# Second block of a channel mixer in seven products, with its first down product moved ahead of it

## The chip, the cores and the metric

The kernel runs on one core of one Trainium2 chip. The metric is the device time of one execution in microseconds (us); a median of three runs is given. A core has TensorE (matmuls, written PE in the profile; PEld is its weight load), VectorE (DVE), ScalarE (ACT), GpSimd (POOL) and SyncE (SP), which here only issues the loads of weights. The engines run side by side and each takes its instructions in the written order; they meet at semaphores.

## The reference, cut to what matters

The reference is two layers of a hybrid diffusion backbone: a token mixer (retention and neighbourhood attention), then a channel mixer, each behind norms and a modulation. Width is 1024, and 512 latent and 128 context tokens go through the same weights, so 640 tokens in all. The change touches the channel mixer alone:

```
def swiglu(h, wg, wu, wd):
    return (jax.nn.silu(h @ wg) * (h @ wu)) @ wd
...
hf = modulate(rmsnorm(x, n_pre_ffn), sh2, sc2)
return x + g2[:, None, :] * rmsnorm(swiglu(hf, w_ffn_gate, w_ffn_up, w_ffn_down), n_post_ffn)
```

wg and wu are 1024 x 2816, wd is 2816 x 1024.

## The kernel before

**Numbers in two parts.** Every operand of a matmul is a float32 that was split into a rounded high part and a low rest. A product is three matmuls (high by high, high by low, low by high). ScalarE makes the high part of a 128x1024 slab of weights (`split`, L1207) and VectorE the low part (`split`, L1696); both engines do the same for the activations.

**Blocks.** The 2816 hidden channels are cut into 11 blocks of 256. A block needs two gate and two up columns of 128 channels (each 1024 deep, for 640 tokens), then silu(gate) * up, split again into `hidh` and `hidl`, then a down product: five tiles of 128 tokens, each 60/5 = 12 matmuls of 512 columns, added up by VectorE in `mix`. Per block, six slabs of weights come by SyncE's queue: four for gate and up, two for down.

**Columns and sevens.** In the first two blocks (`SEVEN = 2`) each column is done plainly (`column`): 8 chunks of depth, 2 halves of 320 tokens, 3 matmuls, 48 matmuls of 320 columns. In the other nine blocks a pair of columns is done by a Strassen-like scheme (`seven`): seven products of quarters, each 4 x 3 matmuls of 320 columns, 84 in place of 96. `quarters(n, ...)` writes product n of pair r into one of four PSUM banks in turn, so product n+4 needs the bank of product n back: `seven_copied` for product 4 (ScalarE has copied product 0), `seven_added` 1 and 2 for products 5 and 6 (VectorE has added products 1 and 2).

What the seven products need beside the matmuls: three sums of weights per pair (`pair_sums`, VectorE, L2247 to L2252), the high and low parts of both slabs and of the sums (`pair_high` parts 0, 1, 2 on ScalarE, `pair_low` parts 0, 1, 2 on VectorE), and, once per layer, four sums of token quarters (`sum_of_tokens` 0 to 2 and `last_sum_of_tokens` on VectorE, L2191 to L2203; their high parts `token_sums` on ScalarE, L1563; their low parts `low_of_tokens` on VectorE, L1706).

**Order.** The order is written out by hand on each engine. TensorE: the four columns of block 0 (partly before all tokens are there, `first_columns`), the four columns of block 1, down of block 0, then for each later block its two pairs and the down of the block before it. VectorE makes the token sums beside the columns of block 1; the pair sums, low parts and last token sum of pair 0 and the sums of pair 1 stand beside the down of block 0. After the adds and the multiplication that end a pair of pairs (`seven_block`), VectorE's loop over the five down tiles (L2337) holds the low parts of the next pair (after tiles 0, 1 and 2) and the sums of the pair behind it (after tile 3).

The code that says which product waits for what, in `seven`:

```
pe.wait_ge(w_lo[slot[i + 1]], turn_of[i + 1])
pe.wait_ge(ts_ready, 4 * l + 4)
pe.wait_ge(seven_copied, r + 1)
quarters(4, s3, t3_)
pe.wait_ge(seven_added, 7 * r + 1)
quarters(5, a12, b21)
```

Of the kernel before, what the change touches and what calls it, by code (L numbers as in the profile page):

```python
# [7 lines left out]
P = 128  # L8
# [35 lines left out]
SEVEN, SIX = 2, 6  # L44
# [81 lines left out]
def build(nc, x_in, w_main, w_first, w_ada, params, decay, state_in, ctx_k, ctx_v, biases, ccol, cvec,  # L126
# [3 lines left out]
    with ctx:  # L130
# [365 lines left out]
        def _(pe):  # L496
# [189 lines left out]
            for l in range(DEPTH):  # L686
# [291 lines left out]

                def down(b):
                    pe.wait_ge(hid_ready, downs.value(1) * 2)  # L980
                    weights = [slab(512)[1:] for _ in range(2)]
                    for t in range(TILES):
                        u = U.take()
                        U.give(down_tile(u, b, t, weights, True, True))
                    slab_over(2)
                    downs.add()

                def seven(r):
# [31 lines left out]
                    pe.wait_ge(ts_ready, 4 * l + 4)  # L1020
# [4 lines left out]
                    pe.wait_ge(seven_added, 7 * r + 2)  # L1025
                    quarters(6, a22, t4_)
                    slab_done.extend([(seven_done, 7 * (r + 1))] * 2)

                def gate_up(b):
                    if b < SEVEN:  # L1030
                        for _ in range(4):
                            column()
                    else:
                        for n in range(2):
                            seven((b - SEVEN) * 2 + n)
# [161 lines left out]
        def _(act):  # L1197
# [93 lines left out]
            for l in range(DEPTH):  # L1291
# [273 lines left out]
                def gate_up(b, more=4):  # L1565
                    for n in range(2):
                        third = b == 0 and n == 1
                        if third:
                            act.wait_ge(bank_ready, 2 * l + 2)
                        else:  # L1570
                            u = U.get()

                        act.wait_ge(hid_ready, hids.count)
                        if third:
                            act.activation(sig[:, 0:CUT], sc[0][:, 0:CUT], ACT.Silu)
                            act.activation(sig[:, CUT:T], sc[1][:, 0:T - CUT], ACT.Silu).then_inc(bank_free, 1)
                        else:
                            for of, part in whole(u, sig[:, :], b == 0 and n == 0):
                                a = act.activation(part, of, ACT.Silu)
                            U.release(a)  # L1580
                        if more == 4:
                            split()
                        U.add()
                        U.wait_released(1)
                        act.activation(hidh[:, b % 2, n, :], sig[:, :], ACT.Copy).then_inc(hid_hi, 1)
                        hids.add()
                        if more == 4:
                            split()
                        else:
                            if n == 0:  # L1590
                                split(2)
                            token_sums(((0, 1), (3,))[n])

# [20 lines left out]

                def seven_block(b):
# [5 lines left out]
                    split(2)  # L1621
# [18 lines left out]
                gate_up(0)  # L1640
                for b in range(1, FB):
                    if b < SEVEN:
                        gate_up(b, 2 if b == SEVEN - 1 else 4)
                    else:
                        seven_block(b)
                    if b == SEVEN - 1:
                        pair_high(0, 0)
                        for t in range(TILES):
                            u = U.get()
                            U.release(act.activation(mix[:, t, :], flat(u[:, :, :]), ACT.Copy))  # L1650
                            if t == 0:
                                pair_high(0, 1)
                                pair_high(0, 2)
                            if t == 2:
                                token_sums((2,))
                    elif b < FB - 1:
                        U.add(TILES)
# [28 lines left out]
        def _(dve):  # L1686
# [220 lines left out]
            for l in range(DEPTH):  # L1907
# [302 lines left out]
                def gate_up(b, more=4):  # L2210
                    for n in range(2):
                        third = b == 0 and n == 1
                        if not third:
                            U.add()
                        if more == 4:
                            split()
                        elif n == 0:
                            sum_of_tokens(0)
                            sum_of_tokens(1)
                        u = U.get()  # L2220
                        if third:
                            dve.wait_ge(bank_free, 2 * l + 2)
                        else:
                            U.wait_released(1)
                        for part, to in whole(u, sig[:, :], b == 0 and n == 0):
                            a = dve.tensor_tensor(to, part, to, ALU.mult)
# [268 lines left out]
```

## Time and profile before

| what | value |
|---|---|
| median of 3 runs | 2127.77 us (2127.35 to 2129.45) |
| the profiled execution's own time | 2126.99 us |
| its span, first to last instruction | 2125.2 us |
| TensorE busy | 2097.1 us, 99% of the span |
| VectorE busy | 1545.4 us, 73% |
| ScalarE busy | 931.0 us, 44% |
| channel mixer of the first layer, about | 642 to 1060 us |
| channel mixer of the second layer, about | 1687 to 2118 us |

The profile is of one execution, so sums of its durations are made against 2126.99 us; the median lies 0.8 us above that. In a timeline each row has start, duration, engine, line, operation, the tiles written and read, shape and count, and in brackets the idle time before it with what ended it. Starts of matmuls are the pace of TensorE; their printed durations overlap, because they are pipelined.

### The profile page before, as it was taken

How to read it: one execution, taken by the hardware profiler on the slowest of the kernel's cores; microseconds unless marked ns; L12 is line 12 of the kernel's file. 1: busy time of each engine (PE TensorE's matmuls, PEld its weight loads, DVE VectorE, ACT ScalarE, POOL GpSimd, SP SyncE). 2: the span in 40 equal slices, each digit the busy share in tenths (PEclk: the TensorE clock that was granted, in tenths of full speed). 3: DMA queues.
4: the chain of work that ended last, by engine and by line, in shares of the span. 5: the costliest groups of instructions: out<-in, count | busy, mean ns of one | idle time of the engine just before them, and what ended most of it. 6: DMA issues, size and time to landing. Idle time of an engine off the chain costs nothing.

```text
span 2125.2 us, 33748 instructions
## 1 busy us (share of the span) xinstructions
PE 2097.1 (99%) x13874; PEld 1997.5 (94%) x13874; DVE 1545.4 (73%) x2467; ACT 931.0 (44%) x1482; POOL 101.6 (5%) x195
## 2 busy tenths in 40 slices
PE   7999999999999999999999999999999999999998
PEld 6999999899989999999899999999999899999997
DVE  5688767777756787887877776755854668787786
ACT  5655432476344432332475554235744544233332
POOL 0000001110000000000000000001100000000000
PEclk9999999999999999999999999999999999999999
DMA  7334355424333222222433333532233312222223
GB/s 306 113 116 129 105 169 174 143 93 147 101 134 115 80 80 80 80 80 86 162 132 119 110 112 132 168 127 78 86 119 130 129 60 80 80 80 85 95 80 139
DMA packets 63098, 246.05 MB, mean 116 GB/s; under 512 B 7777, under 2 KB 8065, under 8 KB 60257
## 3 DMA queue, kind: packets, MB, share of 16 engines
q1 hardware_dynamic: 42336, 158.55, 21.5%
q0 software_dynamic: 20608, 85.35, 11.4%
q8 instruction: 110, 1.80, 0.4%
q14 instruction: 44, 0.35, 0.1%
HBM read 230.20 MB, written 13.66 MB: 115 GB/s over the span
## 4 chain that ended last, share of the span: by engine, by line
PE 94%; DVE 3%; ACT 2%; DMA 1%; issue 0%; DVEq 0%; SPq 0%
PE unit L501 11%; PE unit L502 11%; PE unit L503 11%; PE unit L513 10%; PE unit L516 10%; PE unit L514 10%; PE sc L501 4%; PE sc L502 4%; PE sc L503 4%; PE tp L501 4%; PE tp L502 4%; PE tp L503 4%; PE tp L860 1%; PE sc L836 1%; PE unit L887 1%; PE unit L886 1%
## 5 line engine op out<-in xcount | busy, mean ns | idle before, releaser
L1696 DVE TENSOR_TENSOR wl<-raw,wh 128x1024 fp32r<-128x1024 f32 x204 | 246.9, 1221 | 127.6 <-ACT wh L1207 125.7
L513 PE MATMUL unit<-hmh,wh 128*128 128x320 f32 x1120 | 337.8, 309 | 0.8 <-DVE vl L1706 0.4
L514 PE MATMUL unit<-hml,wh 128*128 128x320 f32 x1120 | 337.3, 309 | 0.0
L516 PE MATMUL unit<-hmh,wl 128*128 128x320 f32 x1120 | 255.3, 309 | 0.0
L1207 ACT ACTIVATE wh<-raw 128x1024 fp32r<-128x1024 f32 x204 | 210.1, 1050 | 98.7 <-DMA raw<-w_main 98.6
L1798 DVE CUSTOM_DVE_ANT_0 junk<-ada,csb,par 128x1024 f32<-128x1024 f32 x160 | 205.5, 1285 | 28.8 <-DMA ada<-w_ada 9.0
L513 PEld LDWEIGHTS unit<-hmh,wh 128*128 128x128 f32 x1120 | 210.2, 188 | 1.2 <-issue 1.2
L514 PEld LDWEIGHTS unit<-hml,wh 128*128 128x128 f32 x1120 | 210.3, 188 | 0.0
L516 PEld LDWEIGHTS unit<-hmh,wl 128*128 128x128 f32 x1120 | 187.1, 188 | 0.0
L501 PE MATMUL unit<-wh,hmh 128*128 128x256 f32 (+1 forms) x544 | 178.9, 329 | 1.5 <-ACT qks L1321 1.5
L503 PE MATMUL unit<-wh,hml 128*128 128x256 f32 (+1 forms) x544 | 177.9, 327 | 0.0
L502 PE MATMUL unit<-wl,hmh 128*128 128x256 f32 (+1 forms) x544 | 177.8, 327 | 0.0
L501 PE MATMUL unit<-wh,hidh 128*128 128x512 f32 x440 | 171.9, 391 | 1.0 <-ACT mix L1650 1.0
L502 PE MATMUL unit<-wl,hidh 128*128 128x512 f32 x440 | 171.4, 390 | 0.0
L503 PE MATMUL unit<-wh,hidl 128*128 128x512 f32 x440 | 171.2, 389 | 0.0
L501 PE MATMUL unit<-hmh,wh 128*128 128x320 f32 (+2 forms) x384 | 123.5, 322 | 2.2 <-issue 1.1
L503 PE MATMUL unit<-hmh,wl 128*128 128x320 f32 (+2 forms) x384 | 118.7, 309 | 0.0
L502 PE MATMUL unit<-hml,wh 128*128 128x320 f32 (+2 forms) x384 | 118.6, 309 | 0.0
L501 PEld LDWEIGHTS unit<-wh,hmh 128*128 128x128 f32 x544 | 104.4, 192 | 10.3 <-issue 1.8
L503 PEld LDWEIGHTS unit<-wh,hml 128*128 128x128 f32 x544 | 104.4, 192 | 8.8
L502 PEld LDWEIGHTS unit<-wl,hmh 128*128 128x128 f32 x544 | 104.4, 192 | 8.6
L1602 ACT ACTIVATE wh<-raw 128x1024 fp32r<-128x1024 f32 x36 | 38.1, 1058 | 150.1 <-DVE e0w L2252 145.4
(465 smaller groups left out, 5322.9 us busy)
## 6 DMA issues: line engine op xcount, KB each, us to landing
raw<-w_main SPq DMA_DIRECT2D x276, 512.0 KB, 4.0
ada<-w_ada POOLq DMA_DIRECT2D x80, 512.0 KB, 4.3
first<-w_first SPq DMA_DIRECT2D x8, 1024.0 KB, 19.5
x<-x_keep POOLq DMA_DIRECT2D x3, 2560.0 KB, 10.3
bias<-biases POOLq DMA_DIRECT2D x32, 192.0 KB, 2.7
x_keep<-x POOLq DMA_DIRECT2D x10, 512.0 KB, 2.9
bias<-biases POOLq DMA_DIRECT2D x16, 256.0 KB, 4.1
gains<-g_rows POOLq DMA_DIRECT2D x4, 1024.0 KB, 6.0
```

The source lines that it names most:

```text
L501: pe.matmul(out, a[0], b[0], start=first, stop=False)
L502: pe.matmul(out, a[0], b[1], start=False, stop=False)
L503: return pe.matmul(out, a[1], b[0], start=False, stop=last)
L513: pe.matmul(u[:, h, 0:n], a[0], xs[h][0], start=f, stop=False)
L514: pe.matmul(u[:, h, 0:n], a[0], xs[h][1], start=False, stop=False)
L516: mm = pe.matmul(u[:, h, 0:n], a[1], xs[h][0], start=False, stop=z)
L836: pe.matmul(sc[hh][:, 0:n], (nqh, nql)[a][rows[hh], j * P:(j + 1) * P], (nkh, nkl)[b][rows[hh], first * P:first * P + n], start=t == 0, st ...
L860: mm = pe.transpose(tp[hh][:, to * P:(to + 1) * P], s[:, hh, n * P:(n + 1) * P], ident[:, :])
L1207: act.activation(wh[slot[i]][:, :], raw[slot[i]][:, :], ACT.Copy).then_inc(w_hi[slot[i]], 1)
L1602: act.activation(wh[slot[i + 1]][:, :], raw[slot[i + 1]][:, :], ACT.Copy).then_inc(w_hi[slot[i + 1]], 1)
L1696: dve.tensor_tensor(wl[slot[i]][:, :], raw[slot[i]][:, :], f32(wh[slot[i]][:, :]), ALU.subtract)\
L1798: a = dve.tensor_tensor_reduce(junk[:, :], ada[ada_slot[i]][:, :], csb[:, which, :], 1.0, par[:, l, B_ADA + chunk:B_ADA + chunk + 1], ALU. ...
```

## The change

`SEVEN` goes from 2 to 1: block 1 is made by seven products too, in both layers, so only block 0 has columns. The down product of block 0 moves ahead of block 1's pairs and is cut for its first two tiles into two halves of depth (`down_part`), the first of which waits for the first half of the hidden channels alone. Between block 1's pairs and those of block 2 no down product stands any more. ScalarE's and VectorE's program for block 0 is written anew: the token sums, the splits of the down weights, and the sums and parts of pair 0 stand beside block 0's columns and its down product. `low_of_tokens` takes the last two sums in the order 2, 3, and TensorE waits for the fourth low part before product 6 instead of product 4. The order of the slabs in memory follows. Cut to its core, on TensorE:

```
-SEVEN, SIX = 2, 6
+SEVEN, SIX = 1, 6
...
                 def down(b):
+                    weights = [slab(512)[1:] for _ in range(2)]
+                    units = []
+                    for k in range(2 if b == 0 else 0):
+                        pe.wait_ge(hid_ready, downs.value() * 2 + k + 1)
+                        for t in range(2):
+                            if k == 0:
+                                units.append(U.take())
+                                U.add()
+                            mm = down_part(units[t], b, t, k, weights, k == 0, k == 1)
+                            if k == 1:
+                                mm.then_inc(unit_ready, 1)
                     pe.wait_ge(hid_ready, downs.value(1) * 2)
-                    weights = [slab(512)[1:] for _ in range(2)]
-                    for t in range(TILES):
+                    for t in range(2 if b == 0 else 0, TILES):
...
                     pe.wait_ge(w_lo[slot[i + 1]], turn_of[i + 1])
-                    pe.wait_ge(ts_ready, 4 * l + 4)
+                    pe.wait_ge(ts_ready, 4 * l + 3)
                     pe.wait_ge(seven_copied, r + 1)
                     quarters(4, s3, t3_)
                     pe.wait_ge(seven_added, 7 * r + 1)
                     quarters(5, a12, b21)
                     pe.wait_ge(seven_added, 7 * r + 2)
+                    pe.wait_ge(ts_ready, 4 * l + 4)
                     quarters(6, a22, t4_)
...
                 first_columns(2 * l)
                 column()
-                for b in range(1, FB - 1):
+                down(0)
+                gate_up(1)
+                for b in range(2, FB - 1):
                     gate_up(b)
                     down(b - 1)
```

On ScalarE, in the new `first_block` from the first multiplied half on, and in `seven_block`:

```
+                def first_block():
...
+                    act.activation(hidh[:, 0, 0, :], sig[:, :], ACT.Copy).then_inc(hid_hi, 1)
+                    hids.add()
+                    split(2)
...
+                    token_sums((0,))
+                    for part in range(3):
+                        pair_high(0, part)
...
+                    for t in range(TILES):
+                        u = U.get()
+                        U.release(act.activation(mix[:, t, :], flat(u[:, :, :]), ACT.Copy))
+                        if t in (0, 2):
+                            token_sums((t + 1,))
...
                 def seven_block(b):
                     r = (b - SEVEN) * 2
+                    if b == SEVEN:
+                        seven_copy(r)
+                        token_sums((2,))
                     pair_high(r + 1, 0)
-                    seven_copy(r)
+                    if b > SEVEN:
+                        seven_copy(r)
```

On VectorE, the stretch that takes the place of `gate_up`, and the loop behind each block:

```
+                U.add()
+                sum_of_tokens(0)
+                gated(0)
+                split(2)
+                pair_sums(0)
+                pair_low(0, 0)
+                gated(1)
+                sum_of_tokens(1)
+                pair_low(0, 1)
+                sum_of_tokens(2)
+                low_of_tokens((0, 1))
+                pair_low(0, 2)
+                last_sum_of_tokens()
+                low_of_tokens((2, 3))
+                pair_sums(1)
+                U.add(TILES)
+                for b in range(SEVEN, FB):
...
                     for t in range(TILES):
-                        u = U.get()
-                        U.release(dve.tensor_tensor(mix[:, t, :], flat(u[:, :, :]), mix[:, t, :], ALU.add))
+                        if b > SEVEN:
+                            u = U.get()
+                            U.release(dve.tensor_tensor(mix[:, t, :], flat(u[:, :, :]), mix[:, t, :], ALU.add))
                         if t == 3:
                             pair_sums((b + 1 - SEVEN) * 2 + 1)
                         if t in (0, 1, 2):
                             pair_low((b + 1 - SEVEN) * 2, t)
```

`gated(n)` on VectorE is the multiplication by up (L2226 before) and the low part of hidden half n (L1706).

## Rows read from the trace of the kernel before

**Rows 1.** The page: span, and busy time of an engine with its share and instructions.

```profile
span 2125.2 us, 33748 instructions
...
PE 2097.1 (99%) x13874; PEld 1997.5 (94%) x13874; DVE 1545.4 (73%) x2467; ACT 931.0 (44%) x1482; POOL 101.6 (5%) x195
```

**Rows 2.** Waits of PE from 640 to 1060 us: total, times, longest (us).

```profile
PE unit L501 <- ACT mix L1650: 0.5, 1, 0.5
```

**Rows 3.** Stretches: length, busy time and count of PE, PEld, DVE, ACT, POOL; clock, DMA.

```profile
664.89:671.93 7.04, 7.04 (x50) 7.04 (x49) 2.42 (x2) 1.71 (x3) 0.00 (x0) 1.00 0.03 12
714.50:739.13 24.63, 24.63 (x169) 24.63 (x168) 17.92 (x26) 9.38 (x11) 0.00 (x0) 1.00 0.26 86
739.13:752.78 13.65, 13.65 (x63) 11.29 (x62) 13.24 (x15) 4.87 (x5) 0.00 (x0) 1.00 0.23 78
```

**Rows 4.** Timeline of DVE beside the columns of block 0, first layer.

```profile
662.22 0.89 DVE L2226 TENSOR_TENSOR sig<-unit,sig 128x384 f32<-128x384 f32 x2
...
673.76 0.82 DVE L1706 TENSOR_TENSOR hidl<-sig,hidh 128x640 fp32r<-128x640 f32 x1 [0.80 <-ACT hidh L1585]
```

**Rows 5.** Timeline of DVE, token sums and the first pairs, first layer.

```profile
691.07 1.48 DVE L2191 TENSOR_TENSOR t4w<-hmh,t2w 128x1280 f32<-128x1280 f32 x1
...
694.21 1.49 DVE L1706 TENSOR_TENSOR t1l<-t1w,t1h 128x1280 fp32r<-128x1280 f32 x1
695.62 1.49 DVE L1706 TENSOR_TENSOR t2l<-t2w,t2h 128x1280 fp32r<-128x1280 f32 x1
...
705.40 1.49 DVE L2200 TENSOR_TENSOR hmh_w<-hmh 128x1280 f32<-128x1280 f32 x1
...
709.77 2.36 DVE L1706 TENSOR_TENSOR wl<-raw,wh 128x1024 fp32r<-128x1024 f32 x2
712.04 1.75 DVE L1706 TENSOR_TENSOR e0l<-e0w,e0h 128x1536 fp32r<-128x1536 f32 x1
713.71 1.49 DVE L1706 TENSOR_TENSOR t4l<-t4w,t4h 128x1280 fp32r<-128x1280 f32 x1
...
716.51 0.69 DVE L2247 TENSOR_TENSOR e1w<-raw 128x512 f32<-128x512 f32 x1
...
719.38 2.39 DVE L1706 TENSOR_TENSOR wl<-raw,wh 128x1024 fp32r<-128x1024 f32 x2
721.69 0.48 DVE L2275 TENSOR_TENSOR u<-sc,c 128x320 f32<-128x320 f32 x1
722.09 1.75 DVE L1706 TENSOR_TENSOR e1l<-e1w,e1h 128x1536 fp32r<-128x1536 f32 x1
```

**Rows 6.** Timeline of ACT, high part of the last token sum.

```profile
709.89 1.28 ACT L1563 ACTIVATE hmh<-hml_w 128x1280 fp32r<-128x1280 f32 x1
```

**Rows 7.** Timelines of PE, DVE and ACT where block 2 ends, first layer.

```profile
739.13 0.39 PE L501 MATMUL unit<-wh,hidh 128*128 128x512 f32 x1
...
741.31 1.56 DVE L2312 TENSOR_TENSOR sig<-usum,sig 128x640 f32<-128x640 f32 x2
742.78 1.22 DVE L2337 TENSOR_TENSOR mix<-unit,mix 128x1024 f32<-128x1024 f32 x1
...
743.55 1.47 ACT L1604 ACTIVATE e0h<-e0w 128x1536 fp32r<-128x1536 f32 x1
```

**Rows 8.** Timeline of PE: the start, and its longest later idle time.

```profile
8.31 1.94 PE L567 MATMUL sc<-ident,xu 128*128 128x128 f32 x8 [8.31 <-DVE xu L1736]
...
14.64 1.75 PE L567 MATMUL tp<-ident,xu 128*128 128x128 f32 x8
16.35 1.09 PE L567 MATMUL sc<-ident,xu 128*128 128x128 f32 x8
...
1060.90 1.09 PE L567 MATMUL sc<-ident,xs 128*128 128x128 f32 x8 [1.91 <-ACT xs L1683]
```

**Rows 9.** Stretches after the last matmul, columns as in rows 3.

```profile
2117.90:2122.00 4.10, 0.00 (x0) 0.00 (x0) 3.74 (x4) 1.44 (x3) 0.00 (x0) 1.00 0.23 95
2122.10:2125.20 3.10, 0.00 (x0) 0.00 (x0) 0.06 (x1) 0.00 (x0) 0.00 (x0) 0.50 0.42 169
```

More of the change, by code:

```diff
@@ L977, in down_tile, with down_part @@
                     return mm
-                def down(b):
+                def down_part(u, b, t, k, weights, first, last):
+                    for n in range(2):
+                        hi, lo = weights[n]
+                        mm = product(u[:, n, :], [m[:, b % 2, k, t * P:(t + 1) * P] for m in (hidh, hidl)],
+                                     (hi[:, k, :], lo[:, k, :]), first, last)
+                    return mm
+                def down(b):
+                    weights = [slab(512)[1:] for _ in range(2)]
[9 more added lines that the diff above has]
+                                mm.then_inc(unit_ready, 1)
                     pe.wait_ge(hid_ready, downs.value(1) * 2)
-                    weights = [slab(512)[1:] for _ in range(2)]
-                    for t in range(TILES):
+                    for t in range(2 if b == 0 else 0, TILES):
                         u = U.take()
@@ L1029, in gate_up @@
                 def gate_up(b):
[L1030 to L1035, printed above, removed]
+                    for n in range(2):
+                        seven((b - SEVEN) * 2 + n)
                 first_columns(2 * l)
                 column()
-                for b in range(1, FB - 1):
+                down(0)
+                gate_up(1)
+                for b in range(2, FB - 1):
                     gate_up(b)
@@ L1563, in token_sums @@
                         act.activation(tsum[n][0], whole_sums[n], ACT.Copy).then_inc(ts_hi, 1)
[L1565 to L1570, printed above, removed]
-                            u = U.get()
[L1573 to L1592, printed above, removed]
                 def pair_high(r, part):
@@ L1638, in seven_block @@
                         pair_high(r + 2, 2)
[L1640 to L1656, printed above, removed]
+                first_block()
+                for b in range(SEVEN, FB):
+                    seven_block(b)
+                    if SEVEN < b < FB - 1:
                         U.add(TILES)
@@ L2208, in low_of_tokens @@
                         lo(tsum[n][1], whole_sums[n], tsum[n][0]).then_inc(ts_ready, 1)
[L2210 to L2226, printed above, removed]
-                        U.release(a)
-                        hids.add()
-                        dve.wait_ge(hid_hi, hids.count)
-                        lo(hidl[:, b % 2, n, :], sig[:, :], hidh[:, b % 2, n, :]).then_inc(hid_ready, 1)
-                        if more == 4:
-                            split()
-                        elif n == 0:
-                            split(2)
-                            sum_of_tokens(2)
-                            low_of_tokens((0, 1))
                 def pair_sums(r):
-                    i = l * PER_LAYER + 4 + W_O + KD + 6 * (SEVEN - 1) + 6 * (r // 2) + 2 * (r % 2)
+                    i = l * PER_LAYER + W_O + KD + (6 if r < 2 else 4 + 6 * (r // 2)) + 2 * (r % 2)
                     if r >= 2:
@@ L2292, in seven_block @@
                         seven_add(i, 2, u2, u4[:, :], 1)
-                        if g == 1:
+                        if g == 1 and b > SEVEN:
                             split()
@@ L2298, in seven_block @@
                         seven_add(i, 3, u4, to[0][:, HALF:T], 2)
-                        if g == 1:
+                        if g == 1 and b > SEVEN:
                             split()
@@ L2405, in main_slabs @@
     down = [slabs_of(w_fd[b * 256:(b + 1) * 256], 512, 2) for b in range(FB)]
-    parts.append(gate_up[0])
-    for b in range(1, FB - 1):
+    parts += [gate_up[0], down[0], gate_up[1]]
+    for b in range(2, FB - 1):
         parts += [gate_up[b], down[b - 1]]
```

47 lines of the change are left out of this document (30 added, 17 removed).

## The prediction

> **What bounds the kernel now.** I read the page first: TensorE is busy for 2097.1 of 2125.2 us [rows 1]. A share is an average, so I went to the stage of the change. The waits of TensorE in the channel mixer of the first layer are one, of 0.5 us [rows 2]; the second layer has the same one and the same pattern, shifted in time. So the mixer is as long as its matmuls, and a matmul that is saved is saved from the end, while a wait that is made is added to it. The stretches give the pace [rows 3]: a column of 48 matmuls takes 7.04 us (0.147 us each), two sevens of 168 matmuls 24.63 us, a down product of 60 wide matmuls 13.65 us. In the same table VectorE is busy for 17.92 us of 24.63 beside a pair of sevens, and for 13.24 of 13.65 beside the down product. That second number is the one to watch: what VectorE does for the next block it does beside the down product, and the change moves one of these away from between two blocks. Everything below is therefore a race of VectorE's written order against TensorE's, and it is done with the timelines of both.
>
> **The matmuls that go.** Block 1 took four columns, 4 x 7.04 = 28.16 us; as sevens it takes 24.63 [rows 3]: 3.53 us less per layer. The wait of 0.5 us was for ScalarE to free a unit beside the old place of the down product [rows 2]. In the new order ScalarE has one copy to do in the 1.4 us before that unit is needed, so I take it as gone: 4.0 us per layer, 8.1 in all.
>
> **The new start of block 0's down.** TensorE ends the last column at 671.93 (end of the first stretch of rows 3). VectorE has by then a new load ahead of the second hidden half: the first token sum fits into idle time before the first multiplication (which stands at 662.22 and starts when TensorE is ready [rows 4]), then come two splits and the sums and first low part of pair 0, about 6.4 us after the first half is done; I find it free just ahead of 672. Then the second half runs as before: its low part at 673.76 for 0.82 us [rows 4], so 674.58. The two first quarters of the down product (12 of its 60 matmuls, 2.7 us) cover 671.93 to 674.66. This wait is closed at 0 to 0.1 us; the down product ends at 671.93 + 13.65 = 685.58, and block 1's first pair starts there.
>
> **Wait A: VectorE's backlog ahead of product 5.** From 674.66 on VectorE has this in its written order, each from start to start in [rows 5]: second token sum, two steps, 694.21 - 691.07 = 3.14; low part of a slab, 1.15 (two are 2.31 from 719.38 to 721.69); third token sum 3.14; two low parts of sums, 2 x 1.41 (694.21 to 695.62); low part of the three weight sums 1.67 (712.04 to 713.71); last token sum 4.37 (705.40 to 709.77). Sum 16.3, so 690.95. Now the new wait: the low part of the last sum needs ScalarE's high part, 1.28 us [rows 6], which cannot start sooner; VectorE stands until 692.35, and queued behind that wait are a second low part, the weight sums of the next pair and its low parts, and behind them the adds that free banks. 692.35 + 2 x 1.41 = 695.17, + 2.87 for the weight sums (716.51 to 719.38) = 698.04, + 2.31 for two low parts = 700.35, + 0.48 for the first add = 700.83. TensorE without waits would be at product 4 at 685.58 + 4 x 1.76 = 692.62 (a product is 24.63 / 14), product 5 at 694.4, product 6 at 696.14. Product 4 waits for the third low part (692.35 + 1.49 = 693.85), 1.2 us; product 5 for the first add, 5.2 us; product 6 for the second add, which stands behind a 1.67 us low part: 700.35 + 0.40 + 1.67 + 0.48 = 702.90, 0.3 us. Product 6 begins at 702.95 instead of 696.14: **6.8 us per layer**. Before, the same low parts and sums lay beside the down product, and the first add stood at 721.69, 7.2 us after the first product at 714.50; the wait needs 8.8.
>
> **Wait B: nothing between block 1 and block 2.** Let X be the moment when TensorE has issued a block's last product. In the trace of before that is 739.13, where the next down product begins [rows 7]. VectorE then still has the last add and two multiplications: these end at 741.31 + 1.56, the next instruction begins at 742.78 [rows 7]. In before that is an add of a down tile, and TensorE is in 13.65 us of down. In the change it is the low part of the very slab that TensorE's next product reads: 742.78 + 1.22 = 744.0, so product 0 of the next pair waits 4.9 us. Product 1 needs the low part of the weight sums, after two slabs and itself: 742.78 + 2 x 1.15 + 1.75 = 746.83 (ScalarE's high part of it is done at 743.55 + 1.47 = 745.02 [rows 7] and is not later), and TensorE could be there at 744.05 + 1.76 = 745.81: 1.0 us. **6.0 us per layer.** Then VectorE has the sums and low parts of the second pair of block 2 to do, 2.87 + 2.31 us, and its first add ends some 6 us after 746.83, still ahead of product 5 at about 754: no third wait, and from there the blocks repeat as before.
>
> **Loads.** The slabs go to the same places by position; the two pairs of block 1 take places that the first two columns free, long before their use, and those of block 2 places that the down product frees. Nothing queues on them at X. I take 0; the price if a load were late is that of a load, and no row speaks for it.
>
> **Sum with the clock unchanged.** Per layer -4.0 + 6.8 + 6.0 = +8.8, in two layers +17.5: 2126.99 + 17.5 = 2144.5 us.
>
> **The clock.** This change makes four stretches, two per layer, in which TensorE has nothing for 4.9 to 5.2 us. The longest idle time of before after the start is 1.91 us and the transposes behind it run as fast as others [rows 8]. After the last matmul the granted clock stays at its full level (2.4 GHz) for some 4.1 us and is then half of it, 1.2 GHz [rows 9]. So idle times between 1.91 and 4.1 us are not shown, and ours are a little longer than the one that ended in a fall. The price: at the start TensorE begins at 8.31 and eight transposes still take 1.75 us at 14.64 but 1.09 at 16.35 [rows 8]; it worked some 7.7 us at the lower level before it rose, and half of that, 3.85 us, is the most that one fall costs. Between 0 and 3.85 I take the middle, 1.9, since the fall comes near the end of the idle time or not at all; and that two of four idle times see it, since 4.9 is barely over 4.1. That is +3.9: **2148.4, say 2148 us**.
>
> The Trainium skill, page "TensorE: Matmul & The Clock Gate", section "HAM oscillation — how this bites in real kernels", says that a gap between bursts of matmuls that is long enough sends TensorE back to the slow clock and that the next burst starts cold, each time anew. Rows 9 agree that it falls after idleness; no row of this case shows a fall in the middle of the work. By that rule all four gaps would count, and the sum would be that of the first rival below.
>
> **The rivals.**
> (1) Every one of the four idle times costs a full fall: 2144.5 + 4 x 3.85 = 2159.9, less about 2 because the wait of product 1 in B would be met later anyway: 2158. For it: the one idle time of that length in the trace ended in a fall. Against: there the fall came after 4.1 us, so work resumes soon after, and full price needs a recovery as slow as that at the start, whose work was transposes with pauses.
> (2) The clock never falls: 2144.5. For it: the margin of 4.9 over 4.1 us is small, and my ends of matmuls are modelled.
> (3) One of the two waits is not there, because VectorE or ScalarE gets to it earlier than I add up: A alone 2126.99 + 2 x (6.8 - 4.0) = 2132.6, B alone 2131.0. Against: each sum is made of instructions that stand in one engine's order with no freedom.
> (4) Faster: VectorE keeps up, since 13.65 us of down product now cover what lay beside columns. This decides itself where the first add of pair 0 is done by 694.4 and the low part of block 2's first slab by X; then the gain stands whole, 2126.99 - 8.1 = 2118.9. Against: the add is 6.4 us late by my sum, and the low part cannot even begin before block 1's last multiplication.
>
> **How the numbers follow.** Chances: forecast 0.50, (1) 0.10, (2) 0.28, (3) 0.06, (4) 0.04; something in between, within 0.2%, 0.02. The likeliest gives 2148. The range takes in (2) with an error of 2 us below and the forecast with more and dearer falls above, short of (1): 2142 to 2156. About 0.2% (4.3 us) is what a measurement of this kernel can tell from no change. Faster 0.05, within 0.2% 0.04, slower 0.91.
>
> **What would show it.** In the profile of the changed kernel, 48 fewer matmuls of 320 columns on the columns' line, net. Waits of TensorE in each mixer: one of about 5 us before product 5 of the first pair, released by VectorE's add (L2275 in before's lines); one of about 5 us before product 0 of block 2's first pair, released by a low part on VectorE; small ones of 1.2, 1.0 and 0.3 us beside them; none at the start of the early down product. A granted clock under 1.00 just behind these two shows falls, and matmuls of 320 columns at twice 0.147 us how long each lasted. I would be wrong in A if ScalarE's last token sum came before 690, in B if the low part of the slab came before the multiplications, and in both if the waits stand but the end moves less, which would mean that before held idle time that I did not see.

## The result, and the profile after

The changed kernel takes 2151.48 us (median of 4 runs, 2150.77 to 2152.68); the kernel before, run beside it on the same chip, 2127.97 us (4 runs, 2127.35 to 2129.45). The ratio is 1.0111 [1.0098, 1.0124]: 23.5 us slower. The prediction was 2148 us in a range of 2142 to 2156, with a chance of 0.91 for slower.

The page of the profiled execution (2150.8 us), the lines that answer to [rows 1], with the columns' line (L513):

```profile
span 2148.7 us, 33786 instructions
...
PE 2100.7 (98%) x13826; PEld 1998.9 (93%) x13826; DVE 1574.5 (73%) x2515; ACT 939.3 (44%) x1490; POOL 101.6 (5%) x195
...
L513 PE MATMUL unit<-hmh,wh 128*128 128x320 f32 x992 | 299.2, 309 | 0.8 <-DVE vl L1714 0.4
```

The same line of the columns on the page of the kernel before:

```profile
L513 PE MATMUL unit<-hmh,wh 128*128 128x320 f32 x1120 | 337.8, 309 | 0.8 <-DVE vl L1706 0.4
```

The columns have three such lines, so they lose 3 x 128 = 384 matmuls, and the sevens gain 336. TensorE has 48 matmuls fewer than in [rows 1] (13874 - 13826), as it should, and yet it is busy for 3.6 us more, in a span that is 23.5 us longer. Less work that takes longer: either each matmul became slower somewhere, or TensorE stands. Both are true.

The waits of TensorE in the first layer, from 635 to 1080 us (total, times, longest), which answer to [rows 2]:

```profile
PE sc L501 <- DVE u L2255: 4.9, 1, 4.9
PE tp L501 <- DVE wl L1714: 4.8, 1, 4.8
PE sc L567 <- ACT xs L1691: 2.0, 1, 2.0
PE sc L501 <- issue: 0.9, 1, 0.9
```

The two long ones are new. The third stands at the end of the layer, at the transposes for which before waited 1.91 us too [rows 8]; the fourth is new and small. ScalarE's 0.5 us of [rows 2] is gone. The second layer has the same three new waits, with 4.9, 4.8 and 0.9 us.

TensorE's timeline at these places (start, duration, engine, line, operation, tiles, and in brackets the idle time before it):

```profile
694.46 0.38 PE L501 MATMUL sc<-hmh,wh 128*128 128x320 f32 x1 [0.91 <-issue]
...
696.14 0.31 PE L503 MATMUL sc<-hmh,wl 128*128 128x320 f32 x1
701.37 0.63 PE L501 MATMUL sc<-hmh,wh 128*128 128x320 f32 x1 [4.92 <-DVE u L2255]
...
704.20 0.47 PE L502 MATMUL sc<-hml,wh 128*128 128x320 f32 x1
704.47 0.47 PE L503 MATMUL sc<-hmh,wl 128*128 128x320 f32 x1
704.73 0.47 PE L501 MATMUL tp<-t4h,wh 128*128 128x320 f32 x1
...
724.97 0.64 PE L501 MATMUL tp<-hmh,wh 128*128 128x320 f32 x1 [4.76 <-DVE wl L1714]
...
728.16 0.31 PE L501 MATMUL tp<-t2h,e0h 128*128 128x320 f32 x1
728.31 0.31 PE L502 MATMUL tp<-t2l,e0h 128*128 128x320 f32 x1
```

Product 4 of the first pair starts at 694.46, product 5 at 701.37, product 6 at 704.73; product 0 of block 2's first pair starts at 724.97, its product 1 at 728.16. Behind each of the two long waits the matmuls are 0.267 us apart (704.20 to 704.73), later 0.147 us again (728.16 to 728.31).

The stretches (columns as in [rows 3]: length, PE, PEld, DVE, ACT, POOL, granted clock, DMA). First both layers' stage, from the first column of block 0 to the first matmul of block 1's down product; then block 0's down product; then each of the four long waits with the stretch behind it:

```profile
642.57:751.04 108.47, 97.88 (x605) 94.33 (x604) 82.20 (x103) 48.25 (x63) 0.53 (x1) 0.95 0.20 73
1699.21:1807.87 108.66, 98.09 (x605) 94.52 (x604) 82.21 (x103) 48.24 (x63) 0.53 (x1) 0.94 0.20 72
672.52:686.35 13.83, 13.83 (x62) 11.11 (x61) 12.42 (x10) 7.78 (x8) 0.00 (x0) 1.00 0.00 0
696.50:701.30 4.80, 0.00 (x0) 0.00 (x0) 4.62 (x7) 2.43 (x2) 0.00 (x0) 0.93 0.00 0
701.37:707.40 6.03, 6.03 (x23) 6.03 (x23) 3.79 (x6) 0.00 (x0) 0.00 (x0) 0.50 0.00 0
720.30:724.90 4.60, 0.00 (x0) 0.00 (x0) 4.42 (x7) 2.88 (x4) 0.00 (x0) 0.96 0.66 228
724.97:727.81 2.84, 2.84 (x11) 2.84 (x12) 2.84 (x3) 1.91 (x2) 0.00 (x0) 0.50 0.00 0
1753.10:1757.95 4.85, 0.00 (x0) 0.00 (x0) 4.67 (x7) 2.43 (x2) 0.00 (x0) 0.73 0.00 0
1758.01:1762.18 4.17, 4.17 (x16) 4.17 (x17) 3.79 (x6) 0.00 (x0) 0.00 (x0) 0.50 0.00 0
1775.95:1780.68 4.73, 0.04 (x1) 0.00 (x0) 4.48 (x8) 2.89 (x4) 0.00 (x0) 0.85 0.66 222
1780.74:1785.98 5.24, 5.24 (x20) 5.24 (x20) 5.09 (x6) 2.34 (x3) 0.00 (x0) 0.50 0.00 0
```

Before, the same stage was 97.15 us long in both layers (641.98 to 739.13, where [rows 7] begins, and 1687.25 to 1784.40). So it grew by 11.32 and 11.51 us, 22.8 of the 23.5 us. All four waits have a clock under 1.00, and behind all four TensorE runs at 0.50, the lower of its two levels (1.2 GHz), for 2.8 to 6.0 us.

VectorE's timeline shows who makes TensorE wait (rows that answer to [rows 5] and [rows 7]), and ScalarE's the row that answers to [rows 6]:

```profile
690.03 1.49 DVE L2211 TENSOR_TENSOR hml_w<-hmh_w,hml_w 128x1280 f32<-128x1280 f32 x1
692.86 1.49 DVE L1714 TENSOR_TENSOR hml<-hml_w,hmh 128x1280 fp32r<-128x1280 f32 x1 [1.34 <-ACT hmh L1579]
...
700.83 0.48 DVE L2255 TENSOR_TENSOR u<-sc,c 128x320 f32<-128x320 f32 x1
...
722.22 1.56 DVE L2292 TENSOR_TENSOR sig<-usum,sig 128x640 f32<-128x640 f32 x2
723.70 2.35 DVE L1714 TENSOR_TENSOR wl<-raw,wh 128x1024 fp32r<-128x1024 f32 x2
725.97 1.75 DVE L1714 TENSOR_TENSOR e0l<-e0w,e0h 128x1536 fp32r<-128x1536 f32 x1
```

```profile
691.56 1.27 ACT L1579 ACTIVATE hmh<-hml_w 128x1280 fp32r<-128x1280 f32 x1 [2.82 <-DVE hml_w L2211]
```

The add that frees product 5's bank (700.83) ends at 701.31, and product 5 starts at 701.37. The low part of the slab for block 2 (723.70) comes straight behind block 1's multiplications (722.22), and product 0 waits for it. Product 4's idle time is put down to "issue", which names nobody; the row that fits is the low part of the third sum, 692.86 + 1.49 = 694.35, against the start at 694.46.

### The profile page after: what moved, and what is told of

The parts are those of the page before. It is cut to its first block, busy times and chain, and to the rows that moved or that the text cites. A ratio compares the mean times of both kernels' runs of the same rounds, so it can differ in the third digit from the quotient of the medians.

```text
span 2148.7 us, 33786 instructions
## 1 busy us (share of the span) xinstructions
PE 2100.7 (98%) x13826; PEld 1998.9 (93%) x13826; DVE 1574.5 (73%) x2515; ACT 939.3 (44%) x1490; POOL 101.6 (5%) x195
## 4 chain that ended last, share of the span: by engine, by line
PE 92%; DVE 4%; ACT 2%; DVEq 1%; issue 1%; DMA 1%; SPq 0%
PE unit L501 11%; PE unit L502 11%; PE unit L503 11%; PE unit L513 9%; PE unit L514 9%; PE unit L516 9%; PE sc L501 4%; PE sc L502 4%; PE sc L503 4%; PE tp L501 4%; PE tp L502 4%; PE tp L503 4%; PE tp L860 1%; PE sc L836 1%; PE unit L887 1%; PE unit L886 1%
## 5 line engine op out<-in xcount | busy, mean ns | idle before, releaser
L1704 DVE TENSOR_TENSOR wl<-raw,wh 128x1024 fp32r<-128x1024 f32 x196 | 237.0, 1220 | 117.9 <-ACT wh L1223 116.8
L513 PE MATMUL unit<-hmh,wh 128*128 128x320 f32 x992 | 299.2, 309 | 0.8 <-DVE vl L1714 0.4
L514 PE MATMUL unit<-hml,wh 128*128 128x320 f32 x992 | 298.7, 309 | 0.0
L1223 ACT ACTIVATE wh<-raw 128x1024 fp32r<-128x1024 f32 x196 | 201.6, 1050 | 97.8 <-DMA raw<-w_main 97.7
L516 PE MATMUL unit<-hmh,wl 128*128 128x320 f32 x992 | 226.0, 309 | 0.0
L513 PEld LDWEIGHTS unit<-hmh,wh 128*128 128x128 f32 x992 | 186.2, 188 | 1.2 <-issue 1.2
L514 PEld LDWEIGHTS unit<-hml,wh 128*128 128x128 f32 x992 | 186.3, 188 | 0.0
L516 PEld LDWEIGHTS unit<-hmh,wl 128*128 128x128 f32 x992 | 165.9, 188 | 0.0
L1589 ACT ACTIVATE wh<-raw 128x1024 fp32r<-128x1024 f32 x40 | 42.3, 1057 | 184.3 <-DVE e0w L2232 171.6
```

The lines of the kernel that those rows point to most:

```text
L513: pe.matmul(u[:, h, 0:n], a[0], xs[h][0], start=f, stop=False)
L514: pe.matmul(u[:, h, 0:n], a[0], xs[h][1], start=False, stop=False)
L516: mm = pe.matmul(u[:, h, 0:n], a[1], xs[h][0], start=False, stop=z)
L1223: act.activation(wh[slot[i]][:, :], raw[slot[i]][:, :], ACT.Copy).then_inc(w_hi[slot[i]], 1)
L1589: act.activation(wh[slot[i + 1]][:, :], raw[slot[i + 1]][:, :], ACT.Copy).then_inc(w_hi[slot[i + 1]], 1)
L1704: dve.tensor_tensor(wl[slot[i]][:, :], raw[slot[i]][:, :], f32(wh[slot[i]][:, :]), ALU.subtract)\
```

## The experiments

The theory: two backlogs of VectorE, A ahead of product 5 and B ahead of product 0 of the third pair, make TensorE stand, each long enough for the clock to fall; nothing else in the change costs anything. The rivals: part of the loss lies elsewhere in the change (the new start of the down product, loads, the token sums' place), or the clock falls for another reason than the idle time.

The medians, the ratios and the length of the stage in both layers (first column to block 1's down product, read from TensorE's starts; 97.15 before):

| kernel | us | before beside it | ratio | stage, us |
|---|---|---|---|---|
| after | 2151.48 | 2127.97 | 1.0111 [1.0098, 1.0124] | 108.47, 108.66 |
| e1_fill | 2145.11 | 2127.61 | 1.0083 [1.0069, 1.0097] | 105.79, 105.80 |
| e2_A | 2139.74 | 2127.61 | 1.0057 [1.0041, 1.0072] | 103.40, 102.61 |
| e3_B | 2136.35 | 2127.61 | 1.0042 [1.0028, 1.0056] | 101.35, 102.15 |
| e4_AB | 2126.49 | 2127.61 | 0.9995 [0.9986, 1.0003] | 96.55, 96.83 |
| e5_pool | 2128.72 | 2127.46 | 1.0006 [0.9997, 1.0015] | 98.26, 96.96 |
| e6_early | 2121.65 | 2127.54 | 0.9971 [0.9960, 0.9982] | 94.03, 94.02 |
| e7_early2 | 2123.58 | 2127.54 | 0.9981 [0.9972, 0.9990] | 94.98, 94.97 |

All diffs below are against the changed kernel unless the text says otherwise.

**e1_fill: the waits stay, but TensorE works in them.** Matmuls whose result nobody reads stand ahead of the two long waits, so the clock alone is taken out.

```diff
+                    def fill(n):
+                        u = U.take()
+                        for _ in range(n):
+                            pe.matmul(u[:, 0, 0:HALF], wh[slot[i - 2]][:, 0:P], hmh[:, 0, 0:HALF], start=True, stop=True)
...
+                    if third_pair:
+                        fill(26)
                     pe.wait_ge(w_lo[slot[i]], turn_of[i])
...
                     quarters(4, s3, t3_)
+                    if first_pair:
+                        fill(28)
                     pe.wait_ge(seven_added, 7 * r + 1)
                     quarters(5, a12, b21)
```

> The changed kernel with matmuls that are thrown away put into the idle time of TensorE: 28 of 320 columns ahead of the wait of product 5 of a layer's first pair, 26 ahead of the wait of product 0 of its third pair; 0.147 us each, so 4.1 and 3.8 us inside waits of 4.9 and 4.8 us. The waits themselves stay. Theory (the two waits of about 5 us per layer cost 0.9 + 4.9 + 4.8 us, and each lets the granted clock fall to 0.5, which costs some 3 us net per layer more): the granted clock is 1.00 from start to end of the mixers, no matmul takes twice 0.147 us there, and the time falls from 2151.5 by 6 to 2145.5 us, between 2144 and 2147. Rival (the clock costs nothing net because VectorE sets the pace of that stretch anyway): the time stays at 2150 to 2152.

Measured: 2145.11 us. The stretch of 120 us around the waits, and the waits in it:

```profile
640.00:760.00 120.00, 116.52 (x722) 109.97 (x722) 95.30 (x117) 53.72 (x69) 0.53 (x1) 1.00 0.23 83
```

```profile
PE tp L501 <- DVE wl L1725: 0.9, 1, 0.9
PE sc L501 <- issue: 0.9, 1, 0.9
PE sc L501 <- DVE u L2266: 0.8, 1, 0.8
PE tp L501 <- DVE e0l L1725: 0.8, 1, 0.8
```

The clock is 1.00 throughout, and the kernel 6.4 us faster than the changed one, though TensorE does more. Against the kernel before that ran beside it, it is 2145.11 - 2127.61 = 17.5 us slower: that is what the two backlogs alone make, less what the sevens save. The clock's part of the 23.5 us is the rest, about 6.0. The last row is new: product 1 waits for the low part of the weight sums. In the changed kernel that low part ends at 725.97 + 1.75 = 727.72, but product 0 at the lower level takes until 728.16, so nothing is seen of the wait.

**e2_A: VectorE's order for the first pair alone.** The second pair's weight sums go ahead of the third token sum's low part, where VectorE stands for ScalarE. The fourth sum's low part, which product 6 needs, goes behind the first add; the second pair's low parts go behind the third.

```diff
-                    for part in (0, 1):
+                    for part in (0, 1) if b > SEVEN else ():
                         pair_low(r + 1, part)
...
                         seven_add(i, 1, c1[i % 2], u2[:, :], 0)
-                        if g == 0:
+                        if g == 0 and b > SEVEN:
                             pair_low(r + 1, 2)
+                        elif g == 0:
+                            low_of_tokens((3,))
...
                         seven_add(i, 3, u4, to[0][:, HALF:T], 2)
+                        if g == 0 and b == SEVEN:
+                            for part in range(3):
+                                pair_low(r + 1, part)
...
-                low_of_tokens((2, 3))
                 pair_sums(1)
+                low_of_tokens((2,))
```

> The changed kernel with another order on VectorE for a layer's first pair alone: the weight sums of the second pair go into the gap in which VectorE waits for ScalarE's high part of the last token sum, and the three adds that free banks go ahead of the second pair's low parts. Same instructions, same counts. Theory (wait A is VectorE's written order, a backlog that ends about 702 us in the first layer): the 4.9 us wait ahead of product 5 goes, what is left is a wait of about 2.7 us ahead of product 4 and 0.3 later, so A falls from 6.8 to 3.0 us per layer, its fall of the clock (1.7 us net per layer) goes too, B stays: 2151.5 - 2 x (3.8 + 1.7) = 2140.5 us, between 2139 and 2142. Rival (ScalarE's late high part of the last token sum sets A): the wait moves to product 6 or to the next pair and the time stays above 2147.

Measured: 2139.74 us. The waits of A shrink to one of 2.2 us ahead of product 4 (in the second layer also 0.3 ahead of product 1 of the second pair); B stays at 4.8. The stage is 0.8 us longer in the first layer than in the second, and the trace says why. The first matmul behind the 2.2 us in both layers, and the stretch behind it:

```profile
697.01 0.61 PE L501 MATMUL sc<-hmh,wh 128*128 128x320 f32 x1 [2.18 <-issue]
...
1748.80 0.38 PE L501 MATMUL sc<-hmh,wh 128*128 128x320 f32 x1 [2.22 <-issue]
```

```profile
696.90:700.20 3.30, 3.19 (x12) 3.22 (x13) 3.20 (x6) 1.08 (x1) 0.00 (x0) 0.50 0.00 0
1748.80:1752.00 3.20, 3.20 (x22) 3.20 (x23) 3.10 (x5) 0.97 (x1) 0.00 (x0) 1.00 0.00 0
```

The same idle time was followed by the lower level in one layer and by the full one in the other.

**e3_B: the third pair's sums and parts alone.** They move from behind block 1's multiplications into VectorE's idle times beside the second pair, and ScalarE makes the third high part before the hidden halves.

```diff
-                        for part in (0, 1):
+                        for part in (0, 1) if b > SEVEN else (0, 1, 2):
                             pair_high(r + 2, part)
...
+                        if g == 1 and b == SEVEN:
+                            pair_sums(r + 2)
                         seven_add(i, 1, c1[i % 2], u2[:, :], 0)
+                        if g == 1 and b == SEVEN:
+                            pair_low(r + 2, 0)
...
                         seven_add(i, 2, u2, u4[:, :], 1)
                         if g == 1 and b > SEVEN:
                             split()
+                        elif g == 1:
+                            pair_low(r + 2, 1)
...
-                        if t in (0, 1, 2):
+                        if t in (0, 1, 2) and b > SEVEN:
                             pair_low((b + 1 - SEVEN) * 2, t)
```

> The changed kernel with the weight sums and the low parts of the third pair (first pair of block 2) moved on VectorE, and its third high part on ScalarE, into the idle time that VectorE has beside the second pair's products. Same instructions, same counts. Theory (wait B is only the order: that work stands behind the last add and the multiplications of block 1 without need): the waits ahead of products 0 and 1 of block 2's first pair go, 6.0 us per layer, and the fall of the clock behind them, 1.4 us net per layer; A stays: 2151.5 - 2 x 7.4 = 2136.7 us, between 2135 and 2139. Rival (VectorE has no room: the work only moves the wait into the second pair or to product 5 of the third): some 3 us per layer or more come back, and the time stays above 2142.

Measured: 2136.35 us. The waits in the stage that are left are those of A:

```profile
PE sc L501 <- DVE u L2255: 4.9, 1, 4.9
...
PE sc L501 <- issue: 0.9, 1, 0.9
```

B needs no fast VectorE, only another order: beside the second pair VectorE has the time for it.

**e4_AB: both.** The lines of the two diffs above, together, and nothing else.

> Both new orders together. Theory: nothing is left but A's 3.0 us per layer against the 4.0 us per layer that the saved matmuls and the old wait give back: 2128.0 - 2 x 1.0 = 2126 us, between 2124.5 and 2128, granted clock 1.00 throughout the mixers, which is a gain that can hardly be told from no change. Rival (the two waits are one backlog, and taking one away lengthens the other): clearly above the 2126 that the two single gains add up to, 2130 or more.

Measured: 2126.49 us, no change that can be measured against before. Two waits are left per layer, 2.2 us ahead of product 4 and 0.3 us ahead of product 1 of the second pair:

```profile
PE sc L501 <- issue: 2.2, 1, 2.2
PE sc L501 <- DVE u L2255: 0.3, 1, 0.3
```

So A and B with the clock behind them carry all of the loss (2151.48 - 2126.49 = 25.0 us), and what the sevens save is eaten by what is left: product 4 waits for the third token sum's low part. Part of that wait is made by the new order itself. In the changed kernel it was 0.9 us; here the low part stands behind the second pair's weight sums and starts at 694.32, though ScalarE's high part is done at 691.70 + 1.28 = 692.98. So some 1.3 of the 2.2 us come from this place, and the rest from the length of VectorE's work ahead of it. No run puts the weight sums behind that low part.

**e5_pool: the second and third token sum on GpSimd.** On top of e4_AB; it should take 2 x 3.14 us [rows 5] from VectorE.

```diff
+                g.wait_ge(ts_full, 4 * l + 1)
+                for to, of, a, b in ((whole_sums[1], whole_sums[0], h22, l22), (whole_sums[3], whole_sums[1], h21, l21)):
+                    g.tensor_tensor(to, a, of, ALU.subtract)
+                    g.drain()
+                    g.tensor_tensor(to, to, b, ALU.add).then_inc(ts_full, 1)
+                    g.drain()
...
                 gated(1)
-                sum_of_tokens(1)
                 pair_low(0, 1)
-                sum_of_tokens(2)
+                dve.wait_ge(ts_full, 4 * l + 3)
                 low_of_tokens((0, 1))
```

> Both new orders, and the second and third token sum (four additions of 128x1280 per layer) made by GpSimd in place of VectorE, right behind the first one; VectorE waits for both before its first low parts of sums. Theory (what is left of A is nothing but VectorE's backlog, 3.0 us late, and these sums are 2 x 3.14 us of it): the last 2.2 us wait ahead of product 4 goes, the channel mixers are free of waits, and the whole gain of 4.0 us per layer stands: 2127.6 - 8 = 2119.5 us, between 2118 and 2121.5, granted clock 1.00 there. It holds if GpSimd ends its four additions within some 13 us, before VectorE comes to its low parts; an estimate from VectorE's 1.49 us each with twice the time is 12 us. Rival (GpSimd beside VectorE slows VectorE's own instructions, or ends late): the wait ahead of product 4 stays or moves to the early down product, and the time is 2124 or more.

Measured: 2128.72 us; my theory's time was wrong, the rival's right. The four additions take 21.8 us from the first start (662.57) to the last end (684.33), where I gave them 13. GpSimd's timeline, then VectorE's:

```profile
662.57 2.96 POOL L1201 TENSOR_TENSOR t2w<-hmh,t1w 128x1280 f32<-128x1280 f32 x1 [14.39 <-DVE t1w L2205]
674.03 2.91 POOL L1203 TENSOR_TENSOR t2w<-t2w,hml 128x1280 f32<-128x1280 f32 x1 [8.51 <-issue]
677.10 3.30 POOL L1201 TENSOR_TENSOR t4w<-hmh,t2w 128x1280 f32<-128x1280 f32 x1 [0.16 <-issue]
680.55 3.78 POOL L1203 TENSOR_TENSOR t4w<-t4w,hml 128x1280 f32<-128x1280 f32 x1
```

```profile
671.25 1.22 DVE L1722 TENSOR_TENSOR wl<-raw,wh 128x1024 fp32r<-128x1024 f32 x1
...
674.43 3.19 DVE L1722 TENSOR_TENSOR hidl<-sig,hidh 128x640 fp32r<-128x640 f32 x1 [0.81 <-ACT hidh L1631]
677.55 3.94 DVE L1722 TENSOR_TENSOR wl<-raw,wh 128x1024 fp32r<-128x1024 f32 x1
684.36 1.49 DVE L1722 TENSOR_TENSOR t1l<-t1w,t1h 128x1280 fp32r<-128x1280 f32 x1 [2.87 <-POOL t4w L1203]
```

The same low part of a slab takes 1.22 us at 671.25 and 3.94 at 677.55, beside GpSimd's additions; the low part of a hidden half, 0.82 us in [rows 4], takes 3.19, and the early down product now waits 2.2 us for it in the first layer. Behind that wait TensorE runs at 0.50 for some 3 us, so part of this layer's 98.26 us of stage is the clock. In the second layer the down product waits 0.9 us and product 4 still 1.5. GpSimd's second addition, free to go at 665.5, starts 8.51 us later, when VectorE pauses for ScalarE. At the end VectorE waits 2.87 us for GpSimd. The Trainium skill, page "GPSIMD Engine Reference", section "1. Specifications", lists GpSimd's way to SBUF as shared with VectorE, with contention where VectorE's instruction has two inputs there; the slowed instructions have two such inputs, so the trace agrees, and it puts a size on it. The multiplication that runs beside GpSimd's first addition has one input in PSUM and keeps its 0.89 us of [rows 4].

**e6_early: the token sums begin sooner, on VectorE.** On top of e4_AB. On ScalarE and VectorE the splits of the next two slabs move ahead of the last tile's modulation and of the first multiplication, and the second token sum's two steps to ahead of the second multiplication and into the wait for ScalarE behind it.

```diff
+                    if t == TILES:
+                        split()
                     if t >= 1:
                         modulated(t - 1, am2[:, l], mod[:, l, SH2:SH2 + KD])
...
                     hids.add()
+                    if n:
+                        sum_of_tokens(1, (1,))
                     dve.wait_ge(hid_hi, hids.count)
...
                 sum_of_tokens(0)
+                split()
                 gated(0)
-                split(2)
+                split()
                 pair_sums(0)
                 pair_low(0, 0)
+                sum_of_tokens(1, (0,))
                 gated(1)
-                sum_of_tokens(1)
                 pair_low(0, 1)
```

> Both new orders, and work of VectorE pulled into idle time that it has ahead of the early down product: the split of the last column's slab into a gap of 1.2 us before the last tile's modulation, the split of the first down slab ahead of the first multiplication, the first step of the second token sum ahead of the second multiplication and its second step into the 0.8 us in which VectorE waits for ScalarE behind it (ScalarE's two splits move along). Same instructions, same counts. Theory (A's rest is VectorE's backlog and nothing else): VectorE is 3.05 us earlier at the last token sum, the 2.2 us wait ahead of product 4 goes, and the late low part of the second hidden half costs the early down product at most 0.6 us: 2127.5 - 2 x (4.0 - 0.6) = 2120.7 us, between 2119 and 2123. Rival (the wait ahead of product 4 is ScalarE's, which makes the high part of the last sum only after its copy of product 0): that wait keeps 1 us or more, 2124 or more.

Measured: 2121.65 us, 0.9971 [0.9960, 0.9982] of before: this kernel beats both. The stage is 94.03 and 94.02 us long, 3.1 less than before. The only wait of TensorE left in it:

```profile
676.12 0.50 PE L501 MATMUL unit<-wh,hidh 128*128 128x512 f32 x1 [0.49 <-DVE hidl L1715]
```

**e7_early2: as e6_early, with the second step behind the second half's low part.** It is the price of one place in VectorE's order.

```diff
-                    if n:
-                        sum_of_tokens(1, (1,))
...
                 gated(1)
+                sum_of_tokens(1, (1,))
                 pair_low(0, 1)
```

This diff is against e6_early.

> As the one before, but the second step of the second token sum stays behind the second hidden half's low part. Theory: VectorE is 1.5 us earlier at the last token sum, the early down product does not wait, the wait ahead of product 4 falls from 2.2 to about 0.9 us: 2127.5 - 2 x (4.0 - 1.5) = 2122.5 us, between 2121 and 2124.5, that is some 2 us above the one before. Rival as there: 2125 or more.

Measured: 2123.58 us, 1.9 us above e6_early. The early down product no longer waits, but product 4 waits 0.6 us and product 1 of the second pair 0.3, per layer. A step of 1.48 us put where VectorE waits for ScalarE anyway is cheaper than the same step behind it.

## Why the prediction was right, and where it was off

**What bounds the kernel: right.** Both long waits in the stage end with VectorE, and moving instructions in VectorE's order, with the high parts that ScalarE makes for them, took the time from 2151.48 to 2121.65 us.

**The matmuls that go, and the old wait: right.** 48 matmuls fewer. The down product of block 0 took 714.50 - (671.93 + 28.16) = 14.41 us before [rows 3], with its 0.5 us wait, and takes 13.83 now: 0.58 us less where I said 0.5. With 3.53 that is 4.1 per layer for my 4.0.

**The new start of the down product: right.** No wait stands there; 13.83 is 0.18 above the 13.65 us of [rows 3], for 0 to 0.1.

**Wait A: right to 0.1 us.** The profiled execution runs 0.59 us late when the stage begins (642.57 for 641.98), so 0.59 is added to my times. Last token sum ends at 691.54, measured 690.03 + 1.49 = 691.52; third low part at 692.94, measured 692.86; the first add ends at 701.42, measured 701.31, and product 5 starts at 701.37. The written order with durations from before was enough. Product 6's 0.3 us is not seen, since product 5 takes 704.73 - 701.37 = 3.36 us at the lower level instead of 1.76; in e1_fill, at the full level, it is 0.2.

**Wait B: right to 0.1 us.** The low part of the slab starts 3.65 us behind TensorE's last product in my sum (742.78 - 739.13 in [rows 7]); measured from 719.90 + 0.15 = 720.05 to 723.70, 3.65. Product 0 starts at 724.97, 4.92 behind that, for my 4.9. The low part of the weight sums is done at 725.97 + 1.75 = 727.72, or 7.67 behind, for 7.70; the 1.0 us that I gave product 1 is hidden in the changed kernel and shows as 0.8 in e1_fill.

**Loads and a third wait: right.** No row of either in the waits.

**The sum with the clock unchanged: right.** 17.5 us forecast, and 17.5 in e1_fill.

**The clock: the term that was mis-sized.** I let two of four waits end in a fall, at 1.9 us each, 3.9 in all. All four fell. The price of one was about right: the stretches at 0.50 hold 22, 10, 15 and 19 starts of matmuls in 6.03, 2.84, 4.17 and 5.24 us, where each would take 0.147, so they cost 2.8, 1.4, 2.0 and 2.4 us, 2.1 on average. That 1.9 came so near is in part luck, since it was the middle between 0 and 3.85. The sum of the four is 8.6 us, of which some 2.6 would have been waits of 0.3 and 1.0 us per layer anyway; that leaves 6.0, and 23.5 - 17.5 from e1_fill is 6.0 too (5.4 between the two profiled executions, 6.4 between the two medians). The step that failed is the count. I took the one stretch after the last matmul, 4.1 us at the full level [rows 9], for a line that a wait of 4.9 barely passes. But one stretch shows one fall, not how soon another can come: in the second layer's A the clock of the idle stretch is 0.73 on average, so it fell long before the end, and in e2_A an idle time of 2.18 us was enough once. The Trainium skill, page "TensorE: Matmul & The Clock Gate", section "HAM oscillation — how this bites in real kernels", says that the burst behind each such gap starts cold anew; the four of four here agree. My first rival, which had all four, was right in that count and wrong in the price: 3.85 us each is nearly twice what was measured. It was half of the time in which the transposes at the start are slow, and [rows 8] show their pace there but no granted clock, so that the whole time was spent at the lower level is not shown.

**The rest.** Forecast +21.4 us against its own execution (2148.4 - 2126.99), measured +23.5: the other terms made their 17.5, and the clock's 6.0 for 3.9 is the whole difference of 2.1. Rival (4), the gain standing whole, needed another order on VectorE and ScalarE, and e6_early shows how far that goes: 5.9 of the 8.1 us.

## What to carry to other kernels

Where TensorE is the bound, a cheaper product is worth what its preparation leaves: write down the other engine's instructions in their order with their durations from the trace of before, and compare the end of each with the start that needs it; here that gave the ends of both long waits to 0.1 us. An idle time of some 5 us in the middle of matmuls costs more than itself, so count the slower matmuls behind each one too. And before a preparation is given to another engine, look for places in the same engine's order where it waits: moving instructions there turned 1.1% slower into 0.3% faster, while GpSimd's help gave nothing here.

## What the hardware showed that I had not expected

- All four waits of 4.8 to 4.9 us were followed by TensorE's lower level, and so were the four of that length that e2_A (B) and e3_B (A) still have. Of the four waits of 2.2 us ahead of product 4 (both layers of e2_A and of e4_AB) one was, the first layer's of e2_A, with the same work ahead of it as in the second layer; the 2.17 us ahead of the early down product in e5_pool's first layer was too. What decides it is left open.
- At the lower level the matmuls of 320 columns are 0.267 us apart instead of 0.147: 1.8 times, not twice.
- A wait costs more than its printed length. Product 5's is printed as 4.92 us; from the start of the matmul before it (696.14) to its own lie 5.23, which is 5.08 more than the usual 0.147, and the next start is late again. That is why the 2.2 and 0.3 us left in e4_AB cost about 3 us of stage.
- GpSimd's additions and VectorE's subtractions with two inputs in SBUF slow each other: 0.82 to 3.19 us and 1.22 to 3.94 us on VectorE, and a start on GpSimd that came 8.51 us late. The rows fit an engine that stands until the other's instruction is done. GpSimd's additions end at 674.03 + 2.91 = 676.94 and 677.10 + 3.30 = 680.40, and VectorE's two slow instructions end at 677.62 and 681.49, 0.7 and 1.1 us behind them, a little less than the 0.82 and 1.22 us that they take alone.
- The stage began 0.59 us late in the profiled execution of the changed kernel. Its trace has a stretch at the lower level near the kernel's start, where that of before is at the full one (stretches of after, then of before):

```profile
24.80:28.10 3.30, 3.28 (x22) 2.16 (x22) 2.82 (x6) 0.51 (x1) 0.00 (x0) 0.50 1.01 417
```

```profile
25.00:29.00 4.00, 3.09 (x30) 2.24 (x31) 3.50 (x7) 1.36 (x3) 0.00 (x0) 1.00 1.02 424
```

A stretch at the lower level stands there in the profiles of e1_fill, e4_AB, e5_pool, e6_early and e7_early2 too, and none in e2_A and e3_B, in code that none of these edits touches; so it is put down to the execution, not to the change. It is not all that varies: e2_A's execution began the stage 1.84 us later than that of before without it.
